# Gate and up, first tile: B11 and B21 turned first, P1 and P2 ahead of the other turns, products in the order P1 P2 P5 P7 P6 P4 P3

## The reference

```python
x = x + merged @ w_out[l]
xn = rms_norm(x, ffn_norm_g[l])
gate, up = jnp.split(xn @ w_gate_up[l], 2, axis=-1)
x = x + (jax.nn.silu(gate) * up) @ w_down[l]
```

## Time and profile before

| | us |
|---|---|
| median of three runs | 2976.38 |
| the profiled execution | 2974.09 |
| its span | 2972.3 |
| TensorE busy | 2816.8 |
| VectorE busy | 1821.4 |
| ScalarE busy | 1332.4 |
| GpSimd busy | 521.7 |

### The profile page before, as it was taken

The page is one execution under the profiler, slowest core; times in us unless marked ns, Lnnn a source line. Parts: engine busy times, 40 slices in busy tenths (PEclk is TensorE's granted clock), DMA queues, the critical chain, the costliest instruction groups (busy, mean ns, idle before and its releaser), DMA issues.

```text
span 2972.3 us, 34921 instructions
## 1 busy us (share of the span) xinstructions
PE 2816.8 (95%) x13918; PEld 2239.3 (75%) x13918; DVE 1821.4 (61%) x2523; ACT 1332.4 (45%) x1936; POOL 521.7 (18%) x433
## 2 busy tenths in 40 slices
PE   6999998999999999999999999999999489999996
PEld 5777777788778787888887666766888368888885
DVE  4344444788875688642233555554445669999997
ACT  4344433333233455221112666664223257777775
POOL 0011112555454110321000111111000200000000
PEclk8999999999999999999999999999999789999998
DMA  3210122345552995322121111115324569999996
GB/s 107 86 43 29 43 91 86 93 136 152 173 163 87 355 253 166 107 57 64 57 71 39 40 43 36 40 43 163 114 90 163 219 248 391 395 394 397 397 396 237
DMA packets 256549, 465.76 MB, mean 157 GB/s; under 512 B 28876, under 2 KB 135508, under 8 KB 255876
## 3 DMA queue, kind: packets, MB, share of 16 engines
q1 hardware_dynamic: 229712, 377.00, 36.1%
q0 software_dynamic: 26528, 86.50, 9.2%
q10 hardware_dynamic: 148, 0.04, 0.0%
HBM read 409.91 MB, written 53.58 MB: 156 GB/s over the span
## 4 chain that ended last, share of the span: by engine, by line
PE 86%; DVE 7%; DMA 3%; ACT 2%; issue 2%; POOL 1%; ACTq 0%; SPq 0%; POOLq 0%; DVEq 0%
PE PS L129 80%; PE PS L132 5%; DVE m L138 4%; ACT m L135 2%; DVE m L144 1%; DMA m<-in_w_down_dram 1%; DMA m<-in_w_in_dram 1%; DMA m<-h_scratch 0%; ACT L135 0%; DVE m L180 0%; POOL m L138 0%; DVE m L183 0%; DVE m L177 0%; DVE m L147 0%; DVE m L141 0%
## 5 line engine op out<-in xcount | busy, mean ns | idle before, releaser
L129 PE MATMUL PS<-m,m 128*128 128x512 f32 (+6 forms) x12102 | 2630.4, 390 | 49.0 <-DVE m L138 27.6
L129 PEld LDWEIGHTS PS<-m,m 128*128 128x128 f32 (+3 forms) x12102 | 2035.4, 184 | 569.1 <-issue 121.4
L135 ACT ACTIVATE m<-m 128x512 fp32r<-128x512 f32 (+5 forms) x723 | 736.3, 1041 | 823.3 <-PE PS L129 421.7
L138 DVE TENSOR_TENSOR m<-m,m 128x512 fp32r<-128x512 f32 (+7 forms) x714 | 908.7, 1303 | 273.1 <-ACT m L135 228.5
L135 ACT ACTIVATE m<-PS 128x512 f32<-128x512 f32 (+4 forms) x507 | 281.9, 578 | 516.4 <-PE PS L129 344.6
L138 DVE TENSOR_TENSOR m<-PS,m 128x512 fp32r<-128x512 f32 (+1 forms) x356 | 233.2, 684 | 340.8 <-PE PS L129 300.3
L138 POOL TENSOR_TENSOR m<-m,m 128x512 f32<-128x512 f32 (+3 forms) x164 | 260.0, 1588 | 580.3 <-DVE small L147 208.5
L132 PE MATMUL PS<-ident,m 128*128 128x128 f32 x1592 | 225.7, 281 | 82.5 <-DVE m L153 36.0
L132 PEld LDWEIGHTS PS<-ident,m 128*128 128x128 f32 x1592 | 193.9, 145 | 121.2 <-DVE m L153 36.3
L135 ACT ACTIVATE m<-m,small 128x640 f32<-128x640 f32 (+4 forms) x199 | 156.3, 788 | 219.6 <-DVE small L141 154.0
L147 DVE CUSTOM_DVE_ANT_0 m<-PS,m 128x640 f32<-128x640 f32 (+4 forms) x192 | 146.4, 775 | 117.9 <-PE PS L129 117.9
(11 more groups left out here) (82 smaller groups left out, 484.6 us busy)
## 6 DMA issues: line engine op xcount, KB each, us to landing
m<-in_w_exp_gate_dram SPq DMA_DIRECT2D x64, 1024.0 KB, 9.0
m<-in_w_exp_up_dram SPq DMA_DIRECT2D x64, 1024.0 KB, 9.0
m<-in_w_exp_down_dram SPq DMA_DIRECT2D x64, 1024.0 KB, 8.6
m<-in_w_mod_dram SPq DMA_DIRECT2D x48, 512.0 KB, 3.8
m<-in_w_gate_up_dram SPq DMA_DIRECT2D x44, 512.0 KB, 6.4
m<-in_w_in_dram SPq DMA_DIRECT2D x41, 512.0 KB, 4.0
m<-in_w_in_dram SPq DMA_DIRECT2D x12, 1024.0 KB, 5.1
h_scratch<-m POOLq DMA_DIRECT2D x22, 512.0 KB, 3.5
```

Of the source, the lines that this page charges most:

```text
L129: return Unsent() if self.e is None else self.e.matmul(o, l, r, start=first, stop=last, **k)
L135: return Unsent() if self.e is None else self.e.activation(o, i, fn, **k)
L138: return Unsent() if self.e is None else self.e.tensor_tensor(o, a, b, op)
```

## The change

TensorE turns B11 whole, then B21, then issues P1 and P2 at once, then turns T1 and T3, P5, T2, P7, P6, then turns T4 and B22, P4, P3. ScalarE and VectorE follow in that order. VectorE makes all eight low parts of B11 and B21 before it scales tiles 4 to 7 and makes the T1 differences; the low parts of B22 come last instead of first. The low part of tile 1's P1 block goes ahead of U2 in tile 0. Banks of P5, P7 and P6 are kept while T4 and B22 are turned. GpSimd's and SyncE's lists are unchanged.

```diff
--- before.py
+++ after.py
@@ -1662,25 +1662,26 @@
             sp.dma_start(cosT, cos_t).then_inc(*sp.landed("cs_in"))
 
         def ffn_pe(pe):
-            for i in range(4):
-                turn_xn(pe, "B11", i)
-                turn_xn(pe, "B21", i)
-            for i in range(4):
-                turn_xn(pe, "B22", i)
+            for T in ("B11", "B21"):
+                for i in range(4):
+                    turn_xn(pe, T, i)
             gu_product(pe, 0, "P1")
-            for i in range(4):
-                turn_xn(pe, "T1", i)
             gu_product(pe, 0, "P2")
-            for i in range(4):
-                turn_xn(pe, "T3", i)
+            for T in ("T1", "T3"):
+                for i in range(4):
+                    turn_xn(pe, T, i)
+            gu_product(pe, 0, "P5")
             for i in range(4):
                 turn_xn(pe, "T2", i)
             gu_product(pe, 0, "P7")
-            gu_product(pe, 0, "P5")
-            for i in range(4):
-                turn_xn(pe, "T4", i)
-            for P in "P6 P4 P3".split():
-                gu_product(pe, 0, P)
+            gu_product(pe, 0, "P6")
+            pe.kept = tuple(bank_of["gu_acc", 0, P] for P in ("P5", "P7", "P6"))
+            for T in ("T4", "B22"):
+                for i in range(4):
+                    turn_xn(pe, T, i)
+            pe.kept = ()
+            gu_product(pe, 0, "P4")
+            gu_product(pe, 0, "P3")
             for c in range(1, 22):
                 for P in GU_ORDER:
                     gu_product(pe, c, P)
@@ -1715,18 +1716,14 @@
 
         def ffn_act(act):
             root_of(act, ssum[:, 4:8], "x1", 1)
-            for i in range(4):
-                xn_high(act, "B11", i)
-                xn_high(act, "B21", i)
+            for T in ("B11", "B21"):
+                for i in range(4):
+                    xn_high(act, T, i)
             for P in "P5 P4 P3".split():
                 gu_high(act, 0, P)
-            for i in range(4):
-                xn_high(act, "B22", i)
             gu_first(act, 0)
-            for i in range(4):
-                xn_high(act, "T1", i)
             gu_silu0(act, 0)
-            for T in "T3 T2 T4".split():
+            for T in "T1 T3 T2 T4 B22".split():
                 for i in range(4):
                     xn_high(act, T, i)
             act.wait_ge("setup_vec")
@@ -1883,20 +1880,23 @@
             xt1_scale(dve, 2)
             xt1_scale(dve, 3)
             inverse_of(dve, ssum[:, 4:8], rs8[:, 4:8], "x1", 1)
+            for T in ("B11", "B21"):
+                for i in range(4):
+                    xn_low(dve, T, i)
             for i in range(4):
-                xn_low(dve, "B11", i)
-                xn_low(dve, "B21", i)
                 xt1_scale(dve, 4 + i)
                 xn_diff_dve(dve, i)
             for P in "P5 P4 P3".split():
                 gu_low(dve, 0, P)
-            for T in "B22 T1 T3 T2 T4".split():
+            for T in "T1 T3 T2 T4 B22".split():
                 for i in range(4):
                     xn_low(dve, T, i)
             for c in range(22):
                 qs = mod_at(c)
+                if c == 0:
+                    gu_low(dve, 1, "P1")
                 gu_u2(dve, c)
-                for P in "P1 P6 P2".split():
+                for P in "P1 P6 P2".split()[c == 0:]:
                     gu_low(dve, c + 1, P)
                 for q in qs[0:1]:
                     mod_add(dve, q)
```

## The result

The changed kernel takes 2983.1 us (median of seven runs, 2982.03 to 2984.84) against 2974.53 for the kernel before in runs beside it: ratio 1.0031, 95% interval 1.0021 to 1.0041, so some 9 us slower. A second set of eight runs gave 1.0029 (1.0018 to 1.0039). That is on the far side of the 0.2% that the forecast named as no change, and inside its range.

A forecast was written before the change was run, and what follows sets the result against it. The start of P3 of tile 0, and its clock, was taken to set the end, with TensorE 95% busy. Order +3.4, P5's clock +1.25 and P3's +0.75 gave +5.4 on 2976.4: 2981.8 us, range 2976.0 to 2986.0.

The forecast's parts named there:

- the 0.2%: Bound between no change and faster or slower: 5.95 us, about what a measurement of this kernel can tell from no change.
- the forecast: Likeliest case, chance 0.46: VectorE and GpSimd alternate, clock losses under 2.5 us; +3.4 to +5.9, taken as 2981.8 us.
- B11 and B21 first: Start of gate and up: scaling 4 moves to 515.3, P1 starts near 513, P1 and P2 done by 519.8, full clock.
- The sign that P2 is done before 520: Listed among signs that the prediction is right: P1 near 513 and P2 done before 520.
- Hand-overs with GpSimd: Scalings and differences without low parts between: VectorE and GpSimd alternate on SBUF, difference 3 ends 527.95, P5 starts 535.6.
- the list: Hand-counted end times of alternating VectorE and GpSimd operations, from scaling 4 at 516.6 to low P3 at 533.0.
- The shortest case: Faster rival, chance 0.07: the engines don't meet as listed, P5 at 527.5, P3 at 548.5, -4.7 us, 2971.7.
- that of VectorE keeping SBUF at each hand-over: Rival, chance 0.09: GpSimd's T3_3 difference comes at 533.7, P5 held until 534.5; +3.6 with P5's clock, 2980.0.
- From P5 to P3: P3 starts 21.0 us after P5, at 556.6 against 553.20, behind VectorE's queue and C22; +3.4 us at full clock.
- The clock: Low-clock losses: B21's turns 0 (up to 0.7), P5 1.25 and P3 0.75 (each bounded by 0 and 2.8).
- The prediction's other row: Clock reading used for P3's loss: after the wait before 506.69 the granted clock was said to be 0.50.
- The slower case: Rival, chance 0.38: same alternation, clock falls in both waits, P5 and P3 pay; +7.5 (2983.9) up to +9.7.

The follow-up runs named there:

- fill2: Changed kernel with useless transposes and matmuls in TensorE's waits, 19 of them ahead of T3's last turn instead of ahead of P5; ratio to before 1.0014, stretch 110.2 us.
- pool_late: Changed kernel with GpSimd starting its differences only behind VectorE's last T1 difference, T3's four first, then T2's and T4's; ratio to before 1.0005, stretch 109.6 us.
- cover_back: Changed kernel with VectorE's old order of B11 and B21 low parts between scalings and T1 differences; ratio to before 1.0017, stretch 113.0 us.
- changed_again: Changed kernel unaltered, profiled and timed a second time; ratio to the kernel before 1.0029 (1.0018 to 1.0039), stretch 116.3 us.
- fill: Changed kernel with useless transposes and matmuls in TensorE's waits, 13 matmuls directly ahead of P5; ratio to before 1.0019, stretch 112.8 us.
- c22_first: Changed kernel with tile 0's U2, U3 and C22 ahead of tile 1's low parts on VectorE; ratio to before 1.0015, stretch 110.9 us.
- new_order: Changed kernel with GpSimd begun behind the last T1 difference, C22 ahead of tile 1's low parts, B22 turned ahead of T1; ratio to before 0.9991.
- order2: new_order with tile 1's P1 issued ahead of tile 0's P4, and U2, U3 and C22 ahead of T4's low parts; ratio to before 0.9978, stretch 102.5 us.

## Why the prediction was right or wrong, by its steps

**B11 and B21 first: right but for the clock.** P1 came at 515.48 and P2 was done at 522.2, each 2.4 later than said, 1.0 of it ahead of the stretch; scaling 4 started 9.4 us after the first turn, where the sum said 8.6. The sign that P2 is done before 520 failed by this. The missing 0.8 us is the low clock under B21's turns, which the sum took as 0 with a bound of 0.7; in fill2, at full clock, scaling 4 starts 8.6 us after the first turn. The reason given was that 17 transposes had raised the clock in the earlier trace rows. But there they ran without a gap; here B11's first three turns came one by one behind scalings. The clock, low from 508.4, rose only at 515.2, when nearly all of B21 was turned. In fill2, with useless transposes in those gaps, it stayed at 1.00.

**Hand-overs with GpSimd: right to some hundredths.** From the start of scaling 4 (517.14) the list gives difference 3's end 12.66 us later; it was 12.65. The low part of P3 was to end at 17.7, it ended at 17.69. The shortest case (P5 at 527.5) and that of VectorE keeping SBUF at each hand-over fall with this; pool_late and cover_back show the cause from both sides.

**From P5 to P3: right.** The sum was 21.0 us from P5's start at full clock. In fill2, the run at full clock, it is 557.72 - 536.67 = 21.05. In the changed kernel it is 23.4, that is 21.0 and P5's 2.4.

**The clock: the term that was mis-sized, and with it the case.** Taken were 0 + 1.25 + 0.75 = 2.0 us; measured 0.8 + 2.4 + 2.6 = 5.8. P5 was given the price of the old P1, whose 12 matmuls began 2.7 us before the clock rose. P5's loss depends on when the clock rises after it has begun, and both profiles show it rising only as P5 ends. At P5's start the low clock had 5.1 us left, where the row that gave the price had 2.7. For P3 the choice between the two rows should have gone the other way: a wait of 4.2 us has more in common with the stretch in which the clock fell than with the wait of 2.34 in which it stayed. The prediction's other row was misread: ahead of 506.69 the wait was 2.19 us and the clock was still 1.00 at its end; it fell at 507.4, among the turns, before begin. With 3.4 at full clock, 2.55 us of loss decided between no change and slower; each of the last two terms was nearly that large by itself. The slower case had this mechanism and priced it from +5.9 to +9.7; it was given 0.38 and should have had more than the forecast. So of the prediction's two near-even outcomes, no change (0.55) and slower (0.41), the less likely one came. That the time lies well inside the range is partly luck: the sum started from 2976.38, the runs beside it have 2974.53, and 9.2 us on top of 2976.38 would be 2985.6, just under the upper end.

**The Trainium skill's rule on transposes** ("TensorE: Matmul & The Clock Gate", part 4) says that the full clock doesn't engage for them. The clock rose at 515.2 with only turns since 507.73, and in changed_again at 533.1 in a stretch of turns; the rule is not borne out for fp32 turns. Its result for P5 came nearly true all the same (2.4 us against the upper bound of 2.8). In changed_again the cause is another one: the turns did raise the clock, and it fell again in the wait behind them. In the first profile the same 20 turns did not raise it; why, the runs don't show.

**The end.** Nothing after tile 1 is seen to absorb the shift: of the stretch's 9.2 us the medians kept 8.6, and the ratio's interval is 6.2 to 12.2 us.

## What to carry to other kernels

Before operations of VectorE are packed closer, look at what GpSimd does in the gaps: here low parts that read PSUM kept their 0.60 us beside it, while operations with both operands in SBUF and GpSimd's made each other wait (a difference 1.63 us for 0.69), so the low parts between them were cover and not delay. A product moved into a wait is worth only what its engine lacks later; here TensorE was short of operands, not of time, and the move lengthened the chain that makes them. And price a new wait of TensorE with the clock that it loses: the waits of 3.0 and 4.2 us cost 2.4 and 2.6 us more in the matmuls behind them, together more than the 3.4 us of the order itself.

## What the runs showed of the hardware

- VectorE and GpSimd took strict turns in all these traces where both had operands in SBUF: with GpSimd waiting, it goes next even when VectorE's following operation is already queued, and the other way round. A scaling goes from 1.28 to 2.28 or 2.30 us, a difference from 0.69 to 1.63, GpSimd's from 1.27 to 1.7 (behind a difference) or 2.24 (behind a scaling). The Trainium skill ("SBUF — State Buffer", SBUF: two separate sides) has the exclusive lock held for a whole instruction; the traces agree, and add who goes next.
- Useless work in TensorE's waits (23 transposes and four groups of 11, 11, 19 and 15 matmuls, fill2) kept the granted clock at 1.00 over the whole stretch and was worth 5.7 us of it; in fill, 13 matmuls in a bank that came free late made P5 start 2.8 us later than in fill2.
- After a wait of 1.43 us (c22_first), 1.99 (new_order) or 2.34 (before) the clock stayed. After 4.2 it was at 0.50 when the matmuls began again in the two profiles of the changed kernel and in pool_late, and 2.6, 2.7 and 2.3 us were lost behind it; in cover_back it fell 0.9 us after they had begun, and 1.6 us were lost.
- The same order doesn't always get the same clock: order2 and new_order have the same list ahead of P5. In new_order's profile P5 ran at 1.00 (3.00 us), in order2's the clock fell 0.4 us after P5 had begun (4.58 us).
